# Packing values with their remainders into one 128-column operand, and a feed-forward that waits for its norm

## What is computed

```python
def hybrid_layer(x, ...):
    hn = rms_norm(x, norm_g[0])
    nsa_q, k_c, v_c, k_s, v_s, k_w, v_w, nsa_g, sb_q, ... = split_columns(hn @ w_in)
    kc, vc = compress_blocks(k_c, ...), compress_blocks(v_c, ...)      # 31 blocks of keys and values
    y_nsa = nsa_attention(...) @ w_nsa_o   # 8 heads of 64: softmax over kc, and causal softmax over
                                           # k_s and over k_w, each times a gate, summed
    y_sb = stick_breaking_attention(...) @ w_sb_o
    mixed = (gate_a * y_nsa + gate_b * y_sb) @ w_out
    x = x + rms_norm(mixed, norm_g[1])
    hf = rms_norm(x, norm_g[2])
    ff = jnp.square(jax.nn.relu(hf @ w_ff1)) @ w_ff2                   # 1024 -> 4096 -> 1024
    return x + rms_norm(ff, norm_g[3])
```

## Time and profile before

| | |
|---|---|
| median of 3 runs | 3599.83 us (3599.14 to 3599.87) |
| profiled execution, device time | 3602.62 us |
| its span, first to last instruction | 3600.8 us |
| busy: PE, weight loads, DVE, ACT, POOL | 95%, 79%, 52%, 38%, 15% |
| mean granted TensorE clock | 0.98 of full |
| compressed attention, causal attention | 172 to 189.4 us and 189.4 to 284.1 us; again 908 us later |
| feed-forward's first group | 516.9 to some 587 us and 1424.2 to some 1493 us |

### The profile page before, as it was taken

The page is one execution under the profiler, slowest core; times in us unless marked ns, Lnnn a source line. Parts: engine busy times, 40 slices in busy tenths (PEclk is TensorE's granted clock), DMA queues, the critical chain, the costliest instruction groups (busy, mean ns, idle before and its releaser), DMA issues. The chain is left out here.

```text
span 3600.8 us, 46138 instructions
## 1 busy us (share of the span) xinstructions
PE 3417.6 (95%) x17790; PEld 2834.9 (79%) x17790; DVE 1881.0 (52%) x2313; ACT 1354.1 (38%) x1993; POOL 537.2 (15%) x376
## 2 busy tenths in 40 slices
PE   7999989999998998999998999899999999999998
PEld 5776877888777687788876888788888788868887
DVE  5364347777536434777755652533333656655444
ACT  4366234444336623434433443312212344333232
POOL 0031003433103200433311110100000100000000
PEclk9999999999999999999999999999999999999999
DMA  3201323443220123344310001111111011112221
GB/s 132 82 1 60 104 105 140 159 159 114 89 85 1 59 94 117 129 153 151 138 53 18 19 13 71 47 60 69 58 60 69 24 67 52 58 36 90 97 93 70
DMA packets 59473, 287.73 MB, mean 80 GB/s; under 512 B 10816, under 2 KB 12096, under 8 KB 32064
## 3 DMA queue, kind: packets, MB, share of 16 engines
q1 hardware_dynamic: 59328, 285.77, 22.6%
HBM read 283.64 MB, written 2.10 MB: 79 GB/s over the span
## 5 line engine op out<-in xcount | busy, mean ns | idle before, releaser
L162 PE MATMUL ps<-h_hi,w_hi_rest 128*128 128x512 f32 (+1 forms) x1072 | 385.1, 359 | 4.5 <-DVE h_lo L396 4.5
L163 PE MATMUL ps<-h_lo,w_hi_rest 128*128 128x512 f32 (+1 forms) x1072 | 363.3, 354 | 0.0
L1371 POOL TENSOR_TENSOR ada_context<-ada_context,ada_scaled 128x768 f32<-128x768 f32 x112 | 288.3, 2574 | 439.2 <-ACT ada_scaled L1483 434.2
L165 PE MATMUL ps<-h_hi,w_lo_rest 128*128 128x512 f32 (+1 forms) x1072 | 321.9, 355 | 0.0
L151 DVE TENSOR_TENSOR w_lo_mix<-w_raw,w_hi_mix 128x2048 fp32r<-128x2048 f32 x92 | 210.7, 2290 | 190.3 <-ACT w_hi_mix L145 190.3
L162 PE MATMUL ps<-h_hi,w_hi_mix 128*128 128x512 f32 x736 | 290.0, 394 | 14.7 <-DVE h_lo L1544 12.4
L435 POOL TENSOR_TENSOR x<-x,y 128x512 f32<-128x512 f32 (+1 forms) x32 | 62.3, 1947 | 1531.8 <-DVE y L443 1531.8
L163 PE MATMUL ps<-h_lo,w_hi_mix 128*128 128x512 f32 x736 | 288.6, 392 | 0.0
L165 PE MATMUL ps<-h_hi,w_lo_mix 128*128 128x512 f32 x736 | 288.3, 392 | 0.0
L145 ACT ACTIVATE w_hi_rest<-w_raw 128x2048 fp32r<-128x2048 f32 x81 | 154.5, 1909 | 326.7 <-PE ps L165 315.4
L1603 DVE TENSOR_TENSOR y<-ps,y 128x512 f32<-128x512 f32 (+1 forms) x224 | 165.9, 751 | 211.6 <-PE ps L165 211.1
(11 more groups left out here) (405 smaller groups left out, 7502.2 us busy)
## 6 DMA issues: line engine op xcount, KB each, us to landing
w_raw<-in_stream SPq DMA_DIRECT2D x205, 1024.0 KB, 4.9
ada_raw<-in_ada_w SPq DMA_DIRECT2D x128, 384.0 KB, 5.1
cmp_w<-in_cmp_w SPq DMA_DIRECT2D x8, 1024.0 KB, 4.9
mla_raw<-in_stream SPq DMA_DIRECT2D x8, 512.0 KB, 3.6
x<-in_x SPq DMA_DIRECT2D x1, 2048.0 KB, 8.9
out<-x SPq DMA_DIRECT2D x8, 256.0 KB, 2.0
x<-in_ctx SPq DMA_DIRECT2D x1, 1024.0 KB, 11.2
consts<-in_consts SPq DMA_DIRECT2D x1, 768.0 KB, 11.7
```

What stands on the lines that cost most here:

```text
L162: pe.matmul(out, whi, xhi, start=start, stop=False)
L163: pe.matmul(out, whi, xlo, start=False, stop=False)
L165: last = pe.matmul(out, wlo, xhi, start=False, stop=stop)
L1371: pool.tensor_tensor(ada.context, ada.context, ada.scaled[:, j % 2, :], ALU.add).then_inc(m["context"], 1)
```

## The change

**Causal attention.** Values and their remainders lie side by side in one stationary operand of 128 columns (`vp`): output rows 0 to 63 get the products of the hi values, rows 64 to 127 those of the lo values. A part of `values` is two matmuls where it was three (the product lo by lo now comes along). The compressed values are packed likewise (`vcp`, with the probabilities' hi part on 32 partitions and their lo part on the next 32), and enter by one fp32r matmul. At the end of a head the two halves must be added: ACT rounds the lower half out of PSUM (`round_low`, i = 8m+5), PE adds it to the upper half by a matmul with the identity (`fold`, i = 8m+6, behind the values), and only then ACT does `head_high` (i = 8m+7) and DVE `head_low`, now behind `low(8m)` of the head after next.

**Compressed attention.** The transposed probabilities are split: behind each of ACT's eight copies, now rounded, DVE makes the remainder; POOL zeroes the padding and makes the remainders of the compressed values.

**Feed-forward of the first stack.** It takes the other path, that of mlp1: squares, sums, root, spread and normed rows first, then the first tiles; ACT takes the relu and DVE the square. DVE splits the second weight unit (`split_first`) while the norm is computed, ACT no longer does at the end of the output projection.

```diff
@@ stage_compress, stage_cmp_attention
-            dve.tensor_tensor(b.vlo, b.v, b.vhi.bitcast(F32), ALU.subtract)
+            dve.tensor_tensor(b.vp[:, :, :, 64:P], b.v.rearrange("p t (r d) -> p t r d", d=64),
+                              b.vp[:, :, :, 0:64].bitcast(F32), ALU.subtract)
...
+                pe.wait_ge(zeroed, 1)
                 pe.wait_ge(probs, t // 2 + 1)
...
-                    last = pe.transpose(k.ps[0:NC, a:a + P], b.pc[:, t, h, 0:NC], k.c["ident"])
+                    last = pe.transpose(k.ps[0:NCP, a:a + P], b.pc[:, t, h, :], k.c["ident"])
...
+            for t in range(QT):
+                for g in range(2):
+                    dve.wait_ge(copied, 2 * t + g + 1)
+                    dst, src = turned(t, g, low)
+                    hi, _ = turned(t, g, slice(0, NCP))
+                    dve.tensor_tensor(dst, src, hi.bitcast(F32), ALU.subtract)
...
+            act.wait_ge(zeroed, 2)
+            act.activation(b.vcp[0:NC, 0:64], b.vc[0:NC, :], ACT.Copy).then_inc(v_hi, 1)
+            act.activation(b.vcp[NCP:NCP + NC, 0:64], b.vc[0:NC, :], ACT.Copy).then_inc(v_hi, 1)
@@ stage_causal_attention, PE
-                    pe.matmul(k.ps[0:64, bank:bank + 512], b.vc[0:NC, :], b.pct[0:NC, h, :], start=True, stop=True)
+                    pe.matmul(k.ps[:, bank:bank + 512], b.vcp, b.pct[:, h, :], start=True, stop=True)
...
-                pe.matmul(out, vhi, hi[:, j, j * P:SEQ], start=False, stop=True, skip_group_check=True)
-                pe.matmul(out, vlo, hi[:, j, j * P:SEQ], start=False, stop=True, skip_group_check=True)
-                last = pe.matmul(out, vhi, lo[:, j, j * P:SEQ], start=False, stop=True,
+                pe.matmul(out, b.vp[:, j, br, :], hi[:, j, j * P:SEQ], start=False, stop=True, skip_group_check=True)
+                last = pe.matmul(out, b.vp[:, j, br, :], lo[:, j, j * P:SEQ], start=False, stop=True,
                                  skip_group_check=True)
...
+            def fold(h):
+                bank = VALUES + (h % 2) * 512
+                pe.wait_ge(s["rounded"], h + 1)
+                pe.matmul(k.ps[0:64, bank:bank + 512], b.identr[64:P, 64:P], b.low_half[64:P, :], start=False, stop=True,
+                          skip_group_check=True).then_inc(s["folded"], 1)
...
+                if i % (2 * QT) == QT + 2 and i > 2 * QT:
+                    fold(i // (2 * QT) - 1)
@@ DVE
-                if i % (2 * QT) == QT + 2 and i > 2 * QT:
-                    head_low(i // (2 * QT) - 1)
+                if i % (2 * QT) == 0 and i > 2 * QT:
+                    head_low(i // (2 * QT) - 2)
+            head_low(HEADS - 2)
             head_low(HEADS - 1)
@@ ACT
+            def round_low(h):
+                bank = VALUES + (h % 2) * 512
+                act.wait_ge(s["summed"], 2 * h + 2)
+                act.activation(b.low_half[64:P, :], k.ps[64:P, bank:bank + 512], ACT.Copy).then_inc(s["rounded"], 1)
...
                 if i % (2 * QT) == QT + 1 and i > 2 * QT:
+                    round_low(i // (2 * QT) - 1)
+                if i % (2 * QT) == QT + 3 and i > 2 * QT:
                     head_high(i // (2 * QT) - 1)
@@ stage_mlp: every "if behind" branch is taken out, what stays is
+            n_pre.pe_all(pe, 9)
+            unit_ready(pe, k, n0)
+            first_tiles(pe, k, n0, 256, 2, tok, lambda i: normed.pe_wait(pe, i), s["ready"])
...
+            n_pre.act_all(act, res.wait)
+            normed.act(act)
...
+            n_post.dve_all(dve, None if post_norm is None else k.root_cols)
+            res.dve(dve)
+            split_first(dve, k, n0 + 1, 1)
+            n_pre.dve_all(dve)
+            normed.dve(dve)
@@ first_block
-        n = stage_project(nc, k, "wo", stream, n, b.mhi, b.mlo, y, SEQ, UNITS_1, wo_norm, 1, beyond=True)
+        n = stage_project(nc, k, "wo", stream, n, b.mhi, b.mlo, y, SEQ, UNITS_1, wo_norm, 1)
```

More of the change, by code:

```diff
@@ L435, in add, with dve @@
         e.tensor_tensor(self.x[:, t, 0:n.tok], self.x[:, t, 0:n.tok], n.src[:, t, 0:n.tok], ALU.add).then_inc(sem, 1)
-    def dve(self, dve, behind=None):
+    def dve(self, dve):
         n = self.norm
[L439 to L442, removed]
+        for t in range(n.kt):
+            for c0, w, scale in self.parts:
                 dve.scalar_tensor_tensor(n.src[:, t, c0:c0 + w], n.src[:, t, c0:c0 + w], scale[:, t:t + 1],
                                          n.rb[:, c0:c0 + w], ALU.mult, ALU.mult).then_inc(self.scaled, 1)
-            if t % 2 and t < n.kt:
+            if t % 2:
                 self.add(dve, t - 1, self.even)
@@ L755, in stage_cmp_attention, with turned @@
         k.sem(f"ca_{s}") for s in ("scored", "masked", "exp", "probs", "flipped", "chain"))
+    v_hi, v_lo = k.sem("ca_v_hi"), k.sem("ca_v_lo")
+    copied, zeroed = k.sem("ca_copied"), k.sem("ca_zeroed")
+    low = slice(NCP, 2 * NCP)
+    def turned(t, g, rows):
+        a = t * 512 + 2048 * g
+        return (b.pct[rows, 4 * g:4 * g + 4, t * P:(t + 1) * P],
+                k.ps[0:NCP, a:a + 512].rearrange("p (h q) -> p h q", q=P))
     with nc.Block() as block:
@@ L1421, in group @@
                     _, outs = tile_out(k, j % ring, tok)
-                    if first and behind and j == 2:
-                        w = unit_tiles(k, n, 0, KT, 256, 0)
-                        dense_tile(pe, k, outs, w, k.hhi, k.hlo, tok, None, range(0, 3))
-                        n_pre.pe_column_sums(pe)
-                        dense_tile(pe, k, outs, w, k.hhi, k.hlo, tok, None, range(3, 5))
-                        n_pre.pe_rows(pe)
-                        last = dense_tile(pe, k, outs, w, k.hhi, k.hlo, tok, None, range(5, KT))
-                    elif j < T1:
+                    if j < T1:
                         last = dense_tile(pe, k, outs, unit_tiles(k, n, 0, KT, 256, j % 2), k.hhi, k.hlo, tok)
@@ L1465, in _ @@
                 n_post.act_root_columns(act)
-            if behind:
-                for t in range(KT):
-                    res.wait(act, t)
-                    act.activation(k.hhi[:, t, 0:tok], k.x[:, t, 0:tok], ACT.Copy, scale=gains[:, t:t + 1]).then_inc(raw_hi, 1)
-                    n_pre.act_square_behind(act, t)
-                n_pre.act_root_columns(act)
-                act.wait_ge(n_pre.spread, 1)
-                act.activation(root_rows, n_pre.rb, ACT.Copy).then_inc(rows_done, 1)
-            else:
-                n_pre.act_all(act, res.wait)
-                normed.act(act)
+            n_pre.act_all(act, res.wait)
+            normed.act(act)
             def scale_rows(it, j):
@@ L1490, in group @@
                 for j in range(T1):
[L1491 to L1504 removed]
+                    act.wait_ge(s["ready"], (T1 + T2) * it + j + 1)
+                    base, _ = tile_out(k, j % ring, tok)
+                    if j >= 2:
+                        act.wait_ge(s["hid_lo"], T1 * it + j - 1)
+                    act.activation(k.sqt[:, j % 2, 0:tok], k.ps[:, base:base + tok], ACT.Relu).then_inc(s["relu"], 1)
+                    hidden_hi(j)
                     if j % 2:
@@ L1593, in group @@
                         split_lo(dve, k, n0 + j // 2 + 2, it=it, per=4)
-                    if ada and not (behind and j < T1 - 1):
+                    if ada:
                         latent_rows(it, j)
```

114 lines of the change are left out of this document (31 added, 83 removed).

## The result

The changed kernel takes 3614.28 us (median of 6 runs, 3612.57 to 3617.14) beside 3599.68 us of the kernel before in the same session: a ratio of 1.0038, 95% interval 1.0028 to 1.0049, 10 to 18 us slower. The forecast was +5.3. The profiled execution took 3612.90 us, its span 3611.1.

The account below looks back on a forecast made before the run. The attention's ring through PE, ACT, DVE and POOL was taken as the bound, not PE's busy time. Attention +6.2, compressed attention +2.1, feed-forward -3.0 make +5.3 us: 3605 us, whole range 3595 to 3616.

Parts of the forecast that it names:

- the ring: Causal attention: widest tile's path PE, ACT, DVE, ACT, DVE, POOL, PE, one tile at a time; 0.23 us shorter.
- The rival that PE is the bound: Causal attention: all removed PE work counts, a head about 9.5 us, the kernel 3572; 7 in 100.
- The price of 0.23: Causal attention: us from one 512-column value matmul to the next, also taken for the packed compressed values' matmul.
- The fold: Attention's longer unit: PE waits for `round_low`, so 5.75 becomes 5.97 us, +0.22; bounds 5.12 and 6.8.
- the fold is free: Rival, attention's longer unit: ACT ready ahead of PE, unit falls to 5.12, kernel 3595 us; 11 in 100.
- `head_low`: Attention's other unit: stands between widest low and next widest maximum, adds 0.61 us; unit 5.75 against 5.42, +0.33.
- The first head: Causal attention: its short unit gives back 0.2 us per layer.
- The tail: Attention's end: the fold's extra handovers are paid by five value parts a third shorter, 0 us.
- Compressed attention: DVE's subtractions behind ACT's last copies end the stage 1.05 us later; twice, +2.1 us.
- The feed-forward: First stack's openings: 67.0 us from reciprocal to eighth output tile, reciprocal 0.71 earlier; -2.1 and -0.9, together -3.0.
- The term of 0.8: Feed-forward opening: added us because reciprocal to first residual row takes 2.34 here, 1.53 in mlp1.
- The rival of the falling clock: Causal attention: PE's idles make the clock fall once per head, +14 us, or 3619; 20 in 100.

Follow-up runs that it names:

- e5: The changed kernel, unaltered, timed again: 3613.22 us, ratio 1.0040.
- e6: On top of e3, `round_low` and `fold` left out, so the products with the values' remainders are missing: 3582.38 us, ratio 0.9949.
- e3: The changed kernel with `head_low` two steps later, ahead of the 256-wide maximum in place of the widest: 3598.70 us, ratio 0.9990.
- e7: On top of e3, the fold one step later on PE, with `head_high` at i = 8m: 3590.63 us, ratio 0.9975.
- e1: The kernel before with both attention stages of the changed one, its own feed-forward kept: 3619.66 us, ratio 1.0043.
- e10: On top of e7, 12 matmuls whose result nothing reads, behind the compressed attention's last transposes: 3593.43 us, ratio 0.9978.
- e4: On top of e3, the fold two steps later on PE, `head_high` one more behind it: 3591.10 us, ratio 0.9965.
- e9: The changed kernel with the old compressed attention, compressed values by one four-byte matmul of 128 stationary columns: 3606.10 us, ratio 1.0015.
- e11: On top of e7, `head_low` one step later still, between two 128-wide tiles: 3590.07 us, ratio 0.9971.
- e8: On top of e4, the old compressed attention, compressed values by one four-byte matmul of 128 stationary columns: 3603.64 us, ratio 1.0010.
- both late: The changed kernel with `head_low` and the fold each moved to later steps: e4 3591.10, e7 3590.63, e11 3590.07 us.

## Where the forecast held and where not

The time lies in the stated range, near its upper end. The forecast held in direction and in what sets the time, and was too small by 9 us. Its chances leaned to "same" (0.52), and slower came. For the terms below the profiled executions are set side by side. What lies outside the four stretches of the table is 3.0 us apart in two executions of the changed kernel (its own and e5's), and between before and changed it took back 3.4 of a sum of 13.7. So single terms are good to some tenths of a microsecond, their sum only to several.

- **What bounds the kernel.** Right. With the ring 0.23 shorter the forecast had 5.12 for one unit without the fold and 5.14 for the other without `head_low`; e6 shows 5.11 for both. The rival that PE is the bound is out: its work fell, the time rose. The price of 0.23 for a 512-column value matmul holds for a stationary operand of 128 columns too; the packed matmul of the compressed values, booked at the same 0.23, keeps the next one off for 0.43, which lies in PE's waiting:

```profile
288.99 0.39 PE L926 MATMUL ps<-pt_hi,v_pack 128*128 128x512 f32 x1
289.22 0.40 PE L927 MATMUL ps<-pt_lo,v_pack 128*128 128x512 f32 x1
```

- **The fold.** Right mechanism, mis-sized: +0.43 (5.72 to 6.15) in place of +0.22. PE waits for `round_low`, which starts 0.21 behind ACT's read as forecast. Behind the wait lie 0.38 to the next scores, not 0.26, and 1.20 from there to the flips, not 1.10. The rival "the fold is free" is out (e3: 6.15), though it becomes nearly so one step later (e7).
- **`head_low`.** Forecast +0.33 in its unit: right in every other head (5.37 to 5.70), +0.57 in the others (5.51 to 6.08). In these DVE's three operations follow each other at 0.72 and 0.71, in the others at 0.61 and 0.59. Together the steady units are 9.5 us longer over both layers where 6.6 had been forecast, falls of the clock left out.
- **The first head.** 0.93 shorter per layer, not 0.2: the removed matmuls counted in both of its later units (5.82 and 5.36 to 5.14 and 5.11).
- **The tail.** Forecast 0, measured 14.06 for 12.91, +1.15 per layer. From the last value matmul's start to DVE's first copy of the next stage, before 282.16 to 284.23, are 2.07; after 289.22 to 292.40, 3.18. The forecast let the shorter value parts pay for that. By themselves they would: from the last 512-wide scores to the last value matmul e6 takes 9.77 us, the kernel before 10.84. But the changed kernel takes 10.88. The sixth moved `head_low` stands here, directly ahead of the last widest maximum, and costs 0.70 (e3, without it, takes 10.18), and the seventh head's fold takes the other 0.41. Behind the last value matmul the chain is bare, as the timeline of the changed kernel's last head shows:

```profile
289.65 0.59 ACT L1031 ACTIVATE low_half<-ps 64x512 fp32r<-64x512 f32 x1 [1.48 <-PE ps L927]
...
290.30 0.44 PE L936 MATMUL ps<-low_half,ident_r 64*64 64x512 f32 x1 [0.68 <-ACT low_half L1031]
...
290.77 0.59 ACT L1026 ACTIVATE on_hi<-ps 64x512 fp32r<-64x512 f32 x1 [0.53 <-PE ps L936]
```

- **The clock.** The forecast's sum had nothing for it; the rival gave it up to 14 us by one fall per head. It came in three places, 6 us in all. At the attention's start: the first two units take 1.1 and 0.8 us longer (10.17 and 9.30, for 9.04 and 8.49). Inside it: one fall per layer, 0.7 and 0.85; in layer 1 of e5 two, 4.3 together, in layer 2 of e1 two as well. And between the attention and the root 1.2 and 1.3 us: the clock falls twice there before and after, and one of the two falls became longer (layer 1: 0.57 of the clock over 473 to 481 us, for 0.79 over 466 to 474 before; layer 2: 0.57 over 1207 to 1215, for 0.79 over 1192 to 1200). That this last part is the change's doing isn't shown: layer 1 of e5 is without it (232.57 up to the root), and so is layer 2 of e1. The first is the packing's doing: PE is idle between the last transposes and the attention for 2.56 us where it was 1.48,

```profile
191.07 0.76 PE L900 MATMUL ps<-k_hi,q_split 128*128 128x512 f32 x1 [2.56 <-PEq L763]
```

and behind that the next eight microseconds are at 0.50 to 0.68 of the clock in all sixteen layers run with the packing and an empty gap, while e10's full clock shows that filling the gap keeps it. The second comes in all six layers of the changed kernel, e1 and e5, and not in the steady units of e3, e4, e6, e7, e9, e10 and e11. That it comes from PE's waits at the fold (0.82 us idle) and in the unit behind it (0.88 or 1.25) is argued from this alone, and e8 had such a fall without a wait at the fold. The Trainium skill ("TensorE: Matmul & The Clock Gate", section "A second HAM failure mode: psum-queue depth-cycling") says that frequent short idles between groups of matmuls can make the clock swing. The trace agrees in kind, not in size: one or two falls in a layer with six such folds.
- **Compressed attention.** Forecast +1.05 per layer; measured +1.10 and +1.39, of which DVE's tail behind ACT is 1.07 and 1.30. Right.
- **The feed-forward.** Forecast 67.0 us from reciprocal to eighth output tile; measured 66.05 and 66.18. The term of 0.8 for a later first residual row did not come (1.43 from the reciprocal, for 2.34 before). The reciprocal came 0.71 earlier against the root, as forecast. So -3.1 and -1.7 in place of -2.1 and -0.9. A part of it is the clock, which the forecast left out. In the 22 and the next 26 us behind the reciprocal the kernel before had 0.78 and 0.87 in layer 1 and 0.84 and 1.00 in layer 2; the changed one has 0.92 and 1.00 in layer 2, and in layer 1 1.00 throughout:

```profile
526.70:548.70 22.00, 19.07 (x97) 12.63 (x97) 17.56 (x24) 8.36 (x15) 7.75 (x4) 1.00 0.66 239
548.70:574.70 26.00, 25.96 (x115) 20.83 (x114) 22.27 (x23) 15.09 (x19) 8.25 (x3) 1.00 0.12 41
```

In sum over both layers: steady units +9.5, first heads -1.9, tails +2.3, clock in the attention +3.5 and behind it +2.5, compressed attention +2.5, feed-forward -4.7, together +13.7 beside the forecast's 5.3. The excess of 8.4 is made up of 6.0 for the clock, 2.9 for fold and `head_low`, 2.3 for the tails and 0.4 for the compressed attention, less 1.5 from the first heads and 1.7 from the feed-forward. So the step that failed is the attention's: the clock and the tail were booked at nothing, and fold and `head_low` a third too low. That the time still lies in the range is in part luck: the feed-forward and the first heads gave 3.2 us more back than forecast, and without that it would be near 3617, outside of it.

Of the signs named beforehand, `head_low` ahead of the widest maximum, DVE's end behind ACT's and the feed-forward's 67.0 us (within 1 us) came. The pairs take 12.04 us for the 11.7 expected, and PE is idle for 0.82 us at the fold, not 1.3. One sign of a wrong forecast came as well, a clock under 0.95 in the attention: it was 0.94 in layer 1 and 0.95 in layer 2, and 0.90 in layer 1 of e5. The rival of the falling clock, held at 20 in 100, is thus partly true: 3.5 us in the attention in place of its 14.

The kernels with both late (3590 to 3591 us in three variants: e4, e7, e11) beat the kernel before by 0.25 to 0.35% and the changed one by more. Removing value matmuls and packing the compressed ones was worth 0.93 per head (11.15 to 10.22 in e6); the change gave that away to the operations that it set on the ring.

## What to carry to other kernels

Where one tile goes round a ring of engines, an instruction's place in the written order is worth more than its cost: the same 0.6 us of `head_low` cost 0.59 to 0.97 ahead of the widest maximum and nothing two steps on, and a fold that waits for a rounding just issued belongs a step or more behind it. Work removed beside the ring shows up only as waiting, and that waiting can hide a dear instruction (e9) or have to be paid for once the ring is shorter (e8), so parts of such a change are to be priced again after each move. At the ends of a stage nothing hides: count the bare chain there, and the idle time of PE in front of the next stage.

## What the hardware did that was not expected

- A PE idle of 2.56 to 2.88 us behind transposes was followed by 0.50 to 0.68 of the clock over eight microseconds in every one of sixteen layers; an idle of 1.48 to 1.57 by 0.79 to 1.00 in eight. Matmuls without a use in the gap kept it at 1.00 in both layers of e10.
- DVE's operations on 512 columns follow each other at 0.59 to 0.61 us around `head_low` in every other head and at 0.71 to 0.72 in the rest, with the same shapes. The same steps show in the kernel before, behind a 256-wide tile; there every other head is 0.15 us longer too (5.51 for 5.36). The cause was not looked for.
- A four-byte matmul of 31 rows and 512 columns takes 1.12 us (two records) with 128 stationary columns and 1.07 with 64; in the packed form its record is 0.50 us, and the next matmul starts 0.43 behind it, not the 0.23 of the value matmuls.
